# An expert stage in column groups: eight slots of 64 to 160 rows in place of slots of 128

## The reference, cut to what matters

```python
logits = jnp.dot(xt, router_w)                      # 256 x 8
top_val, top_idx = lax.top_k(logits, 2)             # two experts per token
top_w = softmax(top_val)
# rows are sorted by expert; each row meets its expert's weights alone:
ys = (silu(xc @ w_gate[e]) * (xc @ w_up[e])) @ w_down[e]   # 1024 -> 3584 -> 1024
out = zeros.at[token].add(ys * weight)
```

## Time and profile before

| | |
|---|---|
| median of three runs | 1648.16 us |
| the profiled execution's span | 1645.7 us |
| PE busy / PEld busy | 98% / 79% of the span |
| DVE / ACT / POOL busy | 78% / 62% / 3% |
| expert stage, first expert matmul to last down matmul | 561.7 to 1634.4 us |
| DMA traffic | 546.71 MB, mean 332 GB/s |

### The profile page before, as it was taken

One profiled execution on the slowest core, in us unless ns is written; L12 is line 12 of the kernel. 1 busy time (PEld: TensorE's weight loads), 2 busy tenths in 40 slices (PEclk: granted clock), 3 DMA queues, 4 the chain that ended last, 5 costly groups with the idle time before them and its releaser, 6 DMA issues.

```text
span 1645.7 us, 20894 instructions
## 1 busy us (share of the span) xinstructions
PE 1604.9 (98%) x8009; PEld 1306.7 (79%) x8010; DVE 1286.5 (78%) x934; ACT 1017.8 (62%) x748; POOL 48.1 (3%) x74
## 2 busy tenths in 40 slices
PE   6999999999999999999999999999999999999998
PEld 5858888886867888888888888888888888888886
DVE  4968644454966878988898898888889889888887
ACT  2455433442354577777677777768677777777774
POOL 0011000000001020000000000000000000000002
PEclk9999999999999999999999999999999999999999
DMA  9997694458578299999999999999999999999994
GB/s 347 302 355 254 222 389 155 153 192 319 185 310 329 97 366 403 368 374 392 379 378 381 384 380 380 385 371 386 376 381 385 376 385 385 378 382 384 368 394 160
DMA packets 164051, 546.71 MB, mean 332 GB/s; under 512 B 10106, under 2 KB 12226, under 8 KB 158882
## 3 DMA queue, kind: packets, MB, share of 16 engines
q1 hardware_dynamic: 156818, 528.02, 84.4%
q10 hardware_dynamic: 4800, 11.32, 2.0%
q0 software_dynamic: 2384, 6.70, 1.3%
HBM read 528.18 MB, written 15.73 MB: 330 GB/s over the span
## 4 chain that ended last, share of the span: by engine, by line
PE 85%; DVE 7%; DMA 4%; ACT 2%; issue 1%; SPq 1%; POOL 0%; DVEq 0%; POOLq 0%; ACTq 0%
PE ps L1959 26%; PE ps L1961 26%; PE ps L1960 26%; DMA weights<-in_ada_w_dram 2%; DVE raw_lo L1515 2%; PE ps L2259 2%; DMA weights<-in_ffn_w_down_dram 1%; DVE weights_lo L1138 1%; PE ps L1885 1%; PE ps L2040 1%; ACT raw_hi L950 1%; DMA raw<-in_moe_w_down_dram 1%; PE ps L2013 1%; PE ps L2025 1%; DVE mx L1346 1%
## 5 line engine op out<-in xcount | busy, mean ns | idle before, releaser
L1515 DVE TENSOR_TENSOR raw_lo<-raw,raw_hi 128x4096 fp32r<-128x4096 f32 x188 | 830.7, 4424 | 136.6 <-ACT raw_hi L950 134.2
L950 ACT ACTIVATE raw_hi<-raw 128x4096 fp32r<-128x4096 f32 x188 | 683.5, 3635 | 213.0 <-PE ps L1961 200.2
L1959 PE MATMUL ps<-raw_hi,hT_hi 128*128 128x512 f32 x1008 | 395.7, 393 | 2.7 <-DVE raw_lo L1515 1.4
L1961 PE MATMUL ps<-raw_hi,hT_lo 128*128 128x512 f32 x1008 | 392.6, 389 | 0.0
L1960 PE MATMUL ps<-raw_lo,hT_hi 128*128 128x512 f32 x1008 | 392.2, 389 | 0.0
L1959 PEld LDWEIGHTS ps<-raw_hi,hT_hi 128*128 128x128 f32 x1008 | 189.3, 188 | 41.6 <-issue 2.1
L1961 PEld LDWEIGHTS ps<-raw_hi,hT_lo 128*128 128x128 f32 x1008 | 189.2, 188 | 39.7
L1960 PEld LDWEIGHTS ps<-raw_lo,hT_hi 128*128 128x128 f32 x1008 | 189.4, 188 | 38.1
L1959 PE MATMUL ps<-raw_hi,m_actT_hi 128*128 128x512 f32 x504 | 197.1, 391 | 0.4 <-DVE raw_lo L1515 0.4
L1961 PE MATMUL ps<-raw_hi,m_actT_lo 128*128 128x512 f32 x504 | 196.4, 390 | 0.0
L1960 PE MATMUL ps<-raw_lo,m_actT_hi 128*128 128x512 f32 x504 | 196.1, 389 | 0.0
(11 more groups left out here) (237 smaller groups left out, 1341.3 us busy)
## 6 DMA issues: line engine op xcount, KB each, us to landing
raw<-in_moe_w_gate_dram SPq DMA_DIRECT2D x126, 1024.0 KB, 6.5
raw<-in_moe_w_up_dram SPq DMA_DIRECT2D x126, 1024.0 KB, 8.8
raw<-in_moe_w_down_dram SPq DMA_DIRECT2D x126, 1024.0 KB, 8.0
weights<-in_ada_w_dram SPq DMA_DIRECT2D x20, 2048.0 KB, 9.8
weights<-in_ffn_w_gate_dram SPq DMA_DIRECT2D x14, 1024.0 KB, 6.0
weights<-in_ffn_w_up_dram SPq DMA_DIRECT2D x14, 1024.0 KB, 8.9
weights<-in_ffn_w_down_dram SPq DMA_DIRECT2D x7, 2048.0 KB, 10.3
weights<-in_w_in_dram SPq DMA_DIRECT2D x6, 2048.0 KB, 12.6
```

Of the source, the lines that this page charges most:

```text
L950: act.activation(raw_hi[HIGH_OF[p]][:], raw[RAW_OF[p]][:], ACT.Copy).then_inc(m_hi, 1)
L1515: dve.tensor_tensor(raw_lo[r][:], raw[r][:], raw_hi[h][:].bitcast(F32), ALU.subtract).then_inc(m_lo, 1)
L1959: pe.matmul(dst, stat_hi, hi, start=start, stop=False, skip_group_check=True)
L1961: return pe.matmul(dst, stat_lo, hi, start=False, stop=stop, skip_group_check=True)
```

## The change

The expert stage alone is rewritten.

- **Rows.** PE gathers the rows of every slot from SBUF with a 0/1 matrix, in phase 3 of the slot before. The scatter to DRAM, its reload and its transposes are gone.
- **Slots.** There are eight, all unrolled, one per expert. Expert 7 takes slot 0; the others are ranked by their number of rows, and the rank picks the slot. A slot has 64, 96, 128 or 160 rows by its passes: A and B are of 64 rows, X is of 32. Rows beyond a slot's capacity would go to an overflow slot of 128 rows (up to four), which is skipped when there are none.
- **Sums.** Matmuls take the f32 weights and rows as they are, with no split. The stationary operand is 32 rows wide, and four matmuls go to the four column groups (output partitions 0, 32, 64, 96). In passes A and B two groups share one half of the columns, for the two halves of the 64 rows; in pass X all four groups have their own columns.
- **Buffers.** The room of the high parts becomes raw buffers: nine in place of six, eight in the last slot. SP takes the chunks of all slots from one list.
- **ACT and DVE** lose the splitting of weights, rows and activations. They keep silu, product, copies, the modulation, and each slot's output; DVE makes the next slot's 0/1 matrix; ACT issues the output's stores.

Cut to its core:

```diff
-RAWS = 6
+RAWS = 9
+FIRST_USE = (0, 1, 3, 5, 2, 4, 6, 7, 8)
...
+SLOT_RANK = (0, 4, 5, 1, 6, 3, 2, 7)
+SLOT_PASSES = ("AX", "A", "A", "ABX", "A", "AX", "AB", "A")
+OVER_PASSES = "AB"
+PASS_ROWS = {"A": 64, "B": 64, "X": 32}
...
+UNIT_BANKS = {"A": (0, 1), "B": (2, 3), "X": (4,)}
+DOWN_BANK = {"A": 5, "B": 6, "X": 7}
+TURN_AT = {"A": 1, "B": 3, "X": 4}
...
+def chunk_order():
+    order = []
+    for s in range(N_EXP):
+        for n in range(NPH):
+            order += [("gu", s, n, i) for i in range(GU_CHUNKS[n])]
+            if n:
+                order += [("down", s, n - 1, i) for i in range(DOWN_CHUNKS[n - 1])]
+            elif s not in (0, LAST):
+                order += [("down", s - 1, NPH - 1, 0)]
+        if s >= LAST - 1:
+            order += [("down", s, NPH - 1, 0)]
+    return order
...
+            def experts():
+                expert = {0: N_EXP - 1}
+                for kind, s, n, i in chunk_order():
+                    if (kind, s, n, i) == ("gu", LAST, 0, 0):
+                        overflow()
+                    if (kind, s, n, i) == ("gu", LAST, 3, 0):
+                        sp.wait_ge(main.stored, STORED[LAST])
+                        sp.dma_start(done_mark[0:1, :], inv_freq[0:1, 0:1]).then_inc(y_early, 16)
+                    if s not in expert:
+                        sp.wait_ge(table_ready, 1)
+                        r = SLOT_RANK[s]
+                        expert[s] = sp.value_load(table[0:1, 0, r:r + 1], min_val=0, max_val=N_EXP - 1)
+                    g, b, _, prior = CHUNK_PLAN[(kind, s, n, i)]
+                    if prior is None:
+                        first_free(b)
                     else:
+                        sp.wait_ge(main.used, prior + 1)
+                    load_chunk(MainSlot(s), main, expert[s], kind, n, i)
...
+            def silu(sig, z, n):
+                a, b = wide_passes(z.passes), 2 if n < NPH - 1 else 1
+                act.wait_ge(sig.used, z.used("gu", n, GU_CHUNKS[n] - 1))
+                if "X" in z.passes:
+                    act.activation(m_sgX[:, 0:WIDE[n] // 4], ps[:, 4, 0:WIDE[n] // 4], ACT.Silu)
+                act.activation(m_sg.rearrange("p (a b) n -> p a b n", b=2)[:, 0:a, 0:b, :],
+                               pair_banks[:, 0:a, 0:b, 0:HU], ACT.Silu).then_inc(sig.silu, 1)
...
+            def modulated_rows(sig, z, banks):
+                n = sum(PASS_ROWS[c] for c in z.passes)
+                act.wait_ge(sig.gathered, z.s + 1)
+                for k in range(KD):
+                    a = act.activation(hX[:, z.rows_at, k, 0:n], gathered_at(z.passes, banks, k), ACT.Identity,
+                                       bias=modc[:, 1, 3, k:k + 1], scale=A[:, 1, 1, k:k + 1])
+                a.then_inc(sig.rows, 1)
...
-            def chunk_high(s, p):
-                act.wait_ge(m_loaded[RAW_OF[p]], loaded(s, p))
...
-                act.activation(raw_hi[HIGH_OF[p]][:], raw[RAW_OF[p]][:], ACT.Copy).then_inc(m_hi, 1)
...
-            def chunk_low(s, p):
-                r, h = RAW_OF[p], HIGH_OF[p]
-                dve.wait_ge(m_hi, taken(s, p))
-                dve.tensor_tensor(raw_lo[r][:], raw[r][:], raw_hi[h][:].bitcast(F32), ALU.subtract).then_inc(m_lo, 1)
...
+            def gated(sig, z, n):
+                a, b = wide_passes(z.passes), 2 if n < NPH - 1 else 1
+                dve.wait_ge(sig.silu, z.s * NPH + (n + 1))
+                if "X" in z.passes:
+                    w = WIDE[n] // 4
+                    dve.tensor_tensor(m_actX[:, 0:w], m_sgX[:, 0:w], ps[:, 4, w:2 * w], ALU.mult)
+                at = [m.rearrange("p (a b) n -> p a b n", b=2)[:, 0:a, 0:b, :] for m in (m_act, m_sg)]
+                dve.tensor_tensor(at[0], at[1], pair_banks[:, 0:a, 0:b, HU:2 * HU], ALU.mult).then_inc(sig.act, 1)
...
+            def gather(sig, z, banks):
+                n = sum(PASS_ROWS[c] for c in z.passes)
+                pe.wait_ge(sig.pick, z.s + 1)
                 for k in range(KD):
                     for t in range(NT):
+                        mm = pe.matmul(gathered_at(z.passes, banks, k), xn[:, t, k * P:k * P + P], pick[:, t, 0:n],
+                                       start=(t == 0), stop=(t == NT - 1))
+                mm.then_inc(sig.gathered, 1)
+            def unit_sums(sig, z, n, between=None):
                 per = CH // (2 * WIDE[n])
+                parts = [(c, b) for b in range(2 if n < NPH - 1 else 1) for c in z.passes if c != "X"]
+                parts += [("X", 0)] if "X" in z.passes else []
+                for i in range(GU_CHUNKS[n]):
+                    buffer = z.buffer("gu", n, i)
+                    pe.wait_ge(sig.loaded[buffer], z.loaded("gu", n, i))
+                    weights = gu_view(raw[buffer], n)
+                    waited = i > 0 or (n == 0 and (sig is over or z.s == 0))
+                    for c, b in parts:
+                        bank, r = UNIT_BANKS[c][b], pass_row(z.passes, c)
+                        if not waited and bank in TURN_AT.values():
+                            pe.wait_ge(sig.copied, z.s * NPH + n)
+                            waited = True
+                        rows = PASS_ROWS[c]
+                        groups, parts32 = P // rows, rows // 32
+                        w = WIDE[n] // 4 if c == "X" else HU
+                        for kk in range(per):
+                            k = per * i + kk
+                            for q in range(4):
+                                g, at32 = q // parts32, r + 32 * (q % parts32)
+                                at = w * (groups * b + g)
+                                mm = pe.matmul(
+                                    ps[32 * q:32 * q + 32, bank, 0:2 * w].rearrange("p (g n) -> p g n", g=2),
+                                    hX[:, z.rows_at, k, at32:at32 + 32], weights[:, kk, :, at:at + w],
+                                    start=(k == 0), stop=(k == KD - 1), skip_group_check=True)
+                    mm.then_inc(sig.used, 1)
+                    if i == 0 and between is not None:
+                        between()
+            def down_sums(sig, z, n):
+                pe.wait_ge(sig.copied, z.s * NPH + (n + 1))
+                if n == 0 and sig is main and z.s:
+                    pe.wait_ge(sig.y, z.s)
+                for i in range(DOWN_CHUNKS[n]):
+                    buffer = z.buffer("down", n, i)
+                    pe.wait_ge(sig.loaded[buffer], z.loaded("down", n, i))
+                    for c in z.passes:
+                        rows = PASS_ROWS[c]
+                        w = rows * D // P
+                        for j in range(4):
+                            q = 4 * i + j
+                            if c != "X":
+                                stationary = maT[:, c == "B", 2 * i + j % 2, HEAD * (j // 2):HEAD * (j // 2) + HEAD]
+                            elif n < NPH - 1:
+                                stationary = maTX[:, q % 2, 32 * (q // 2):32 * (q // 2) + 32]
+                            else:
+                                stationary = maTX[:, 0, 32 * q:32 * q + 32]
+                            for quarter in range(4):
+                                g, half = quarter // (rows // 32), quarter % (rows // 32)
+                                mm = pe.matmul(ps[32 * quarter:32 * quarter + 32, DOWN_BANK[c], 0:w],
+                                               stationary[:, 32 * half:32 * half + 32],
+                                               raw[buffer][:, D * j + w * g:D * j + w * g + w],
+                                               start=(n == 0 and q == 0), stop=(n == NPH - 1 and j == 3),
+                                               skip_group_check=True)
+                    mm.then_inc(sig.used, 1)
...
+            def slot(s):
+                z = MainSlot(s)
+                def next_rows():
+                    banks = gather_banks(z.passes)
+                    if TURN_AT["B"] in banks and "B" in z.passes:
+                        pe.wait_ge(main.copied, z.s * NPH + 3)
+                    gather(main, MainSlot(s + 1), banks)
+                def last_picks():
+                    pe.wait_ge(pick_last, 1)
+                    for t in range(NT):
+                        mm = pe.transpose(ps[:, 2, t * P:t * P + P], pickw[:, t, :], ident[:])
+                    mm.then_inc(turned_pick, 1)
+                pe.wait_ge(main.rows, s + 1)
+                unit_sums(main, z, 0)
+                if s not in (0, LAST):
+                    down_sums(main, MainSlot(s - 1), NPH - 1)
+                turn_units(main, z, 0)
+                for n in range(1, NPH):
+                    unit_sums(main, z, n, (next_rows if s < LAST else last_picks) if n == NPH - 1 else None)
+                    down_sums(main, z, n - 1)
+                    turn_units(main, z, n)
+                if s >= LAST - 1:
+                    down_sums(main, z, NPH - 1)
```

(63 more changed lines are left out.)

834 lines of the change are left out of this document (361 added, 473 removed).

## The result

Nine slots of 189 chunks became eight of 168, and the kernel takes **1512.09 us** (median; 1507.47 to 1512.6) against 1647.26 (1646.17 to 1648.26) measured beside it: ratio 0.917 [0.916, 0.919], 8.3% faster. The forecast was 1493, the range 1472 to 1550. The profiled execution has a span of 1510.8 us, where 1490.8 was forecast: 20 us more.

What follows compares the result with a forecast made beforehand. PE was taken as the bound, DMA some 7% behind. Slots with allowance (915.9 us) plus 1.9 for the later start made a 917.8 us stage, 154.9 less: span 1490.8, plus 2.5, forecast 1493 us, range 1472 to 1550.

Steps and rivals of the forecast that it cites:

- The set: Expert stage on PE: four f32 matmuls of 512 columns side by side take 0.858 us; 966 of them, 828.8 us.
- The third rival: Expert matmuls: weight loads are not hidden, a set takes 1.076 us, the kernel 1683 us, slower than before; chance 0.07.
- DMA's rate: Expert weight loads: 408 GB/s, so a chunk of 2.10 MB takes 5.14 us and a slot 107.9.
- the second rival: Expert weight loads: DMA stays at 381 GB/s, a chunk takes 5.50 us, the kernel 1505 us; chance 0.12.
- Waits for DMA: Expert stage: PE waits for loads in slot 2 alone, 21 us of that slot's 99.7.
- The check for overflow: Ahead of slot 7: PE's check for overflow slots, with no cover, costs 2 us.
- The clock: Expert stage: PE's granted clock stays at 1.00; under 1.00 in slots 1, 2 or 4 would be a sign of error.
- Transposes and changes between 32 and 128 columns: Expert stage on PE: 161 transposes, 16.1 us, and two width changes in each of 32 phases, 9.6 us.
- Gathers: Inside the expert stage: PE's seven gathers of rows for the next slot, 3.8 us each, 26.6 us.
- Uncovered turns of slots 0 and 7, and the last copy: Silu and product in phase 0 without cover, 2.4 and 1.6 us; the copy before the last down chunk, 1.0.
- The allowance of 6.4 us for small waits: Expert stage: 0.2 us in each of 32 phases, in case down sums hide silu, product and copy less well.
- The first rival: Expert stage: many small waits, 0.3 us more per chunk over 168 chunks, 50 us, 1543 us; chance 0.18.

Runs made afterwards that it cites:

- experiment 8: The changed kernel with the four matmuls of each set written to two column groups, two to each: 2302.78 us, ratio 1.398.
- experiment 4: The changed kernel with one read of the overflow table ahead of the loop on each engine, in place of four: 1503.45 us, ratio 0.914.
- the spread order: The changed kernel with wide slots spread between narrow ones (AX, A, AB, A, ABX, A, AX, A): 1494.27 us, ratio 0.907.
- experiments 2 and 3: The changed kernel with its slots reordered: wide ones spread (2), 1494.27 us, or wide ones together behind slot 0 (3), 1543.08 us.
- experiment 1: The kernel before with its overflow limit raised from 128 to 256 rows, so its ninth slot does not run: 1535.13 us, ratio 0.932.
- after: The changed kernel itself, against the kernel before: 1512.09 us, ratio 0.917.
- experiment 5: The changed kernel with two column groups of 64 columns in passes A and B, in place of four of 32: 1524.12 us, ratio 0.926.

## Why the prediction was right, and where it was off

The mechanism held: eight slots for nine, sets of 0.858 us, PE as the bound but for slot 2. The span came 20.0 us over, because terms beside the sets were mis-sized and one was missing. The terms, measured by the starts of PE's records in the stage:

- **The set: right.** 0.858 us by the earlier trace rows, 0.858 measured, 828.8 us for all; 8 shows that it is four matmuls side by side. The Trainium skill, "TensorE: Matmul & The Clock Gate", Part 3 (Measured speedup), gives 2.38 times for three column tiles, and the estimate from it was 1.08 us for a set; the trace disagrees, with steps of 0.429 us for four column groups as for two. The third rival fell with it.
- **DMA's rate: right.** 408 forecast, 402 to 409 in the slices; the second rival's 381 did not come.
- **Waits for DMA: 32.4 us for 21.2, +11.2** (29.3 of idle, and 3 that the records' ends hide). Slot 2 has 23 of idle for 21. Slot 7 has 6.3, where none was forecast; the table gave that slot 79.3 us and it took 85.5. Two steps of the prediction failed there. It let "eight of nine buffers" be ahead in slot 7 too, where its own list of changes has one buffer less. And it counted nothing but chunks on DMA, where the gather of the output rows moves 2.10 MB beside them. The lead itself was full when slot 7 began.
- **The check for overflow: 7.2 us for 2, +5.2.** Mis-sized; experiment 4 took 5 back.
- **The clock: forecast 1.00; at half for 20.4 us in four stretches, +8.1** on PE's steps (its 16.7 us of work in them would be 8.3 at the full clock). The prediction looked for a cause only in the narrow matmuls of the earlier trace rows, and not in the idle of PE that its own waits made.
- **Transposes and changes between 32 and 128 columns: 27.3 us for 25.7, +1.6**, with two transposes at the end that it left out. A change costs 0.15 us, as forecast.
- **Gathers: 27.7 for 26.6, +1.1.** Uncovered turns of slots 0 and 7, and the last copy: 4.2 for 5.0, -0.8.
- **The allowance of 6.4 us for small waits: 1.8 used, -4.6.** The first rival (0.3 us at every chunk) does not show anywhere. That the allowance paid part of the above is luck.
- **The start: 561.8 for 563.6, -1.8.** The gather ended 1.4 us sooner than the 560.4 taken from the trace before. Over the executions of these kernels with a gap there, the start moved between 561.6 and 563.1 us.

The sum: 11.2 + 5.2 + 8.1 + 1.6 + 1.1 - 0.8 - 4.6 - 1.8 = 20.0 us, the whole difference. Of the prediction's own signs of being wrong one came, a clock under 1.00 in slot 2 (0.98 in its stretch), and the gap was not "only in slot 2".

The sentence that the order "keeps DMA's shortfall to one slot" holds for slots 1 to 6, and still misled: PE waits there for 23 us, and the spread order takes 18 of all waits away. The table that gave the 21 us was not used on other orders; as experiments 2 and 3 show, it would have told.

The share of the ninth slot was in the forecast, but not told apart. Nine slots in 1072.7 us are 119 us each, and experiment 1 puts the ninth at 112 of the 135 us gained. With inputs that send no expert over 128 rows the change would be worth about 23 us, an estimate from experiment 1; with one overflow it loses 30.

## What to carry to other kernels

When PE and DMA are within some per cent of each other, count buffers slot by slot: the order of wide and narrow work decides what PE waits, and a saving on PE is partly handed back as waits for DMA (36 us of work gave 14). Count everything that DMA moves in a slot, not the weights alone. For f32, four column groups of 32 columns have the step of two groups of 64, 0.429 us, and save the changes of width if all passes keep to them. A check that finds nothing still has its price, 7.0 us here, where PE makes it with no work beside it.

## What the runs showed of the hardware

- A step of f32 matmuls of 512 columns takes 0.429 us whether its stationary operands are four of 32 columns (after), two of 64 (experiment 5) or two of 32 (experiment 8). The loads of four different operands, 0.13 us for the four, lie inside the step.
- A change between 64 and 32 columns costs PE about 0.14 us (experiment 5), to 128 and back about 0.15 each (after: four transposes of 0.10 us with their two changes take 0.70 us).
- In the stage the granted clock fell to half at 561.0, 588.3, 789.6 and 1410.9 us, with idle of PE of 2.85, 2.06, 2.03 and 7.02 us ending at 561.8, 587.6, 789.3 and 1413.9. It did not fall behind the 2.17 us that end at 1480.5, nor behind the idle of 1.4 to 1.6 us in slot 2, nor in experiment 5 at idle of 2.85 and 2.04 us: the length of one idle alone doesn't tell. It came back after 3.4 us in two cases and after 6.8 in the other two.
- Loads of weights into SBUF ran at 409 GB/s for as long as they were let, with PE busy beside them. A gather of 2.10 MB by POOL's queue took its share of the same rate: 395 GB/s for both together from 1463 to 1478 us.
